# Hybrid encoder block: from GLU to the end, the low parts of weights and of the second norm's tiles are subtracted on VectorE instead of GpSimd

## The chip, the cores and the metric

The kernel runs on one core of one Trainium2 chip. The metric is the device time of one execution in microseconds, taken as the median of several runs. Everything is float32.

## The reference

One layer of an encoder block on 272 positions (16 meta tokens and 256 inputs) with 2048 features. All the heavy work is matrix products:

```python
hn = rms_norm(h, norm1_g)
q, k, v, u, g_na, g_ssm = split(hn @ w_in)
y_na = neighbourhood_attention(q, k, v, rpb) @ w_proj_na
y = gelu(s5(u)); y_ssm = (y * sigmoid(y @ w_glu)) @ w_proj_ssm
mixed = sigmoid(g_na) * y_na + sigmoid(g_ssm) * y_ssm
h = h + mixed @ w_out
a, g = split(rms_norm(h, norm2_g) @ w_up)
a = a[-1] * conv_w[0] + a[0] * conv_w[1] + a[+1] * conv_w[2] + conv_b   # along positions
h = h + (gelu(a) * g) @ w_down
return rms_norm(h, final_g)[:, 16:]
```

## The kernel before

Activations are kept with features on the partitions. To keep float32 precision every product is made of three: each operand is split into a high part (rounded to `fp32r`) and a low part (the difference), and TensorE adds high x high, low x high and high x low into PSUM.

**Units of weights.** Weights stream through three rings of four slots: `w_raw` (filled by SyncE's DMA queue), `w_hi` (ACT copies, `hi_unit`) and `w_lo` (a subtraction `w_raw - w_hi`, `lo_unit`, line 407). A unit is 128 x 1024 numbers, 512 KB, and takes TensorE 24 matmuls. The rings work like this: the load of a unit waits until the low part of the unit four before it is made (`s_lo`), its high part waits for the load and until TensorE has used the unit four before it (`s_used`), its low part waits for the high part (`s_hi`), and TensorE waits for the low part (`s_lo`). Until the end of attention the subtractions are shared between GpSimd and VectorE; from unit GLU 4 on all are GpSimd's, in the order of the units.

**Stages from GLU to the end**, in units: GLU 8, projections 32 (per half: two units of attention, two of `z`), `w_out` 32, up 176, down 88. `U_GLU`, `U_PROJ`, `U_OUT`, `U_UP`, `U_DOWN` are the numbers of the first units. The products of a stage are drained like this:

- GLU: ACT makes the sigmoid into `glu_ring` (line 879), VectorE multiplies (`mix_ring`, 1242), ACT makes `z_hi` (882), VectorE `z_lo` (1246). In the same stage ACT makes the sigmoids of the gates (872). The second product of the projections waits for all of `z_lo`.
- Projections: per block of four units VectorE makes four products with the gates (1256, 1258), two additions (1262) and, after ACT's high part (891), two subtractions (1266).
- After the last mix ACT starts the reload of the residual `xT` from DRAM (895), and VectorE waits for it (`s_xre`) ahead of its loop over `w_out`.
- `w_out`: per block of four units VectorE adds two tiles onto `xT` (1277), ACT squares them (579), TensorE sums the squares one block later (1371).
- Second norm: VectorE makes 1/rms in `rstd` (956, 961), then the 16 normed tiles in a ring of four (968), ACT the high parts (590), GpSimd the low parts (`norm_lo`, 421). VectorE starts on four tiles when GpSimd is done with the four before.
- Up: per block of eight units (four for the conv branch, four for the gate) ACT starts the conv (918), VectorE adds its two outer taps (1288, 1291), ACT makes gelu (926), VectorE multiplies by the gate (1297), ACT makes the high part (929), VectorE the low part (1302). PSUM holds two blocks, so TensorE waits for the products of line 1297 two blocks back. The down product begins when the last of them is done.

Of the kernel before, what the change touches and what calls it, by code (L numbers as in the profile page):

```python
# [22 lines left out]
SEED = 4  # L23
# [5 lines left out]
LIVE = N_META - 2  # L29
NL = L - LIVE  # L30
KT = D_MODEL // P
KH = HALF // P
FT = D_FF // P
DEPTH = 4
# [29 lines left out]
def encoder_block(nc, x, meta, norm1_g, w_in, rpb, lam_re, lam_im, log_step, b_re, b_im, c_re, c_im,  # L64
# [7 lines left out]
    ds = bass.ds  # L72
# [10 lines left out]
    with ctx:  # L83
# [380 lines left out]
        def _(pool):  # L464
# [85 lines left out]
            with pool.Fori(0, HEADS // 4) as i:  # L550
                for k in range(4):
# [5 lines left out]
                                .then_inc(s_bm, 1)  # L557
                    lo_unit(pool, (U_G + DEPTH + 4 * (G_SCAN + G_SSM)) + 8 * i, 2 * k)
                    lo_unit(pool, (U_G + DEPTH + 4 * (G_SCAN + G_SSM)) + 8 * i, 2 * k + 1)
            for k in range(8):  # L560
                lo_unit(pool, U_GLU + DEPTH, k)
            split_loop(pool, lo_unit, U_PROJ, 4, 8)
            split_loop(pool, lo_unit, U_OUT, 4, 8)
            norm_lo(pool, 1, NL)
            split_loop(pool, lo_unit, U_UP, FT // 4, 16)
            split_loop(pool, lo_unit, U_DOWN, FT // 2 - 1, 4)


        @block.scalar
# [377 lines left out]
        def _(dve):  # L947
# [5 lines left out]
            def norm(which, lo, n):  # L953

                dve.wait_ge(s_ss, which + 1)
                dve.tensor_scalar(rstd[:, 0:n], ps[:, 6, 0:n], 1.0 / D_MODEL, EPS, ALU.mult, ALU.add).then_inc(s_var, 1)
                if which == 0:
                    dve.wait_ge(s_gtp, 1)
                    dve.tensor_copy(gains[:, :], ps[:, 7, 0:2 * KT]).then_inc(s_gcp, 1)
                dve.wait_ge(s_sd, which + 1)  # L960
                dve.reciprocal(rstd[:, 0:n], rstd[:, 0:n])
                dve.drain()
                src = xT if which else x0T
                if which < 2:
                    with dve.Fori(0, KT // DEPTH) as i:
                        for k in range(DEPTH):
                            dve.wait_ge(s_nl, DEPTH * i + (KT * which + SEED))
                            dve.scalar_tensor_tensor(
                                out=tr[:, k, 0:n], in0=src[:, ds(DEPTH * i + k, 1), lo:lo + n].rearrange("p k n -> p (k n)"),
                                scalar=gains[:, ds(DEPTH * i + (KT * which + k), 1)], in1=rstd[:, 0:n],  # L970
                                op0=ALU.mult, op1=ALU.mult).then_inc(s_nt, 1)

            norm(0, 0, L)


# [259 lines left out]
                              anh[:, :, 0:2].bitcast(F), ALU.subtract).then_inc(s_mal, 1)  # L1235


            for n in range(KH):
                dve.wait_ge(s_sg, n + 1)
                if n >= 4:  # L1240
                    dve.wait_ge(s_zl, n - 3)
                dve.tensor_tensor(mt[:, n % 4, :], yT[:, n, LIVE:L], gt[:, n % 4, :], ALU.mult).then_inc(s_z, 1)
                if n % 4 == 3:
                    for m in range(n - 3, n + 1):
                        dve.wait_ge(s_zh, m + 1)
                        dve.tensor_tensor(zl[:, m, :], mt[:, m % 4, :], zh[:, m, :].bitcast(F), ALU.subtract).then_inc(s_zl, 1)
# [3 lines left out]
            dve.wait_ge(s_zl, KH)  # L1250
            with dve.Fori(0, 4) as i:
                for k in range(2):
                    dve.wait_ge(s_used, 8 * i + (U_PROJ + 4 * (k + 1)))
                    for m in range(2):
                        f = 4 * i + (2 * k + m)
# [15 lines left out]
            dve.wait_ge(s_xre, 16)  # L1271
            with dve.Fori(0, 4) as i:
                for k in range(2):
                    dve.wait_ge(s_used, 8 * i + (U_OUT + 4 * (k + 1)))
                    for m in range(2):
                        h = xT[:, ds(4 * i + (2 * k + m), 1), LIVE:L].rearrange("p k n -> p (k n)")
                        last = dve.tensor_tensor(h, h, ps[:, 2 * k + m, 0:NL], ALU.add)
                    last.then_inc(s_h1, 1)
            norm(1, LIVE, NL)


            with dve.Fori(0, FT // 4) as i:
                for k in range(2):
                    for m in range(2):
                        f = 4 * i + (2 * k + m)
                        dve.wait_ge(s_c, f + 1)
                        c = cv[:, k, m, :]
                        dve.scalar_tensor_tensor(out=c, in0=ps[:, 4 * k + m, 1:NL - 1], scalar=cvw[:, ds(f, 1)], in1=c,  # L1288
                                                 op0=ALU.mult, op1=ALU.add)
                        dve.drain()  # L1290
                        dve.scalar_tensor_tensor(out=cv[:, k, m, 0:SEQ - 1], in0=ps[:, 4 * k + m, 3:NL],
                                                 scalar=cvw[:, ds(f + 2 * FT, 1)], in1=cv[:, k, m, 0:SEQ - 1],
                                                 op0=ALU.mult, op1=ALU.add).then_inc(s_cd, 1)
                    dve.wait_ge(s_used, 16 * i + (U_UP + 8 * (k + 1)))
                    for m in range(2):
                        dve.wait_ge(s_ge, 4 * i + (2 * k + m + 1) + SEED)
# [7 lines left out]
                                          ALU.subtract).then_inc(s_fl, 1)  # L1304


            for m in range(0, KT, 2):
                dve.wait_ge(s_used, U_END - 1 if m < KH else U_END)
                h = xT[:, m:m + 2, N_META:L]
                dve.tensor_tensor(h, h, ps[:, m // 2, :].rearrange("p (a b) -> p a b", a=2), ALU.add).then_inc(s_h2, 1)  # L1310
# [388 lines left out]
```

## Time and profile before

| | |
|---|---|
| timed runs | 1756.8 us median of 3 (1756.56 to 1758.4) |
| profiled execution | span 1754.1 us from the first to the last instruction |
| around the span | 2.7 us between the span and the median |
| granted TensorE clock, mean | 0.952 of full speed |
| TensorE matmul busy | 1588.3 us (91%) |
| GpSimd busy | 1228.6 us (70%) |
| ACT busy | 808.9 us (46%) |
| VectorE busy | 595.1 us (34%) |

PE is TensorE, PEld its weight loads, DVE is VectorE, POOL is GpSimd, SP is SyncE. Busy shares are means over stages with different limits. An idle time in brackets is that of the engine ahead of the instruction, with what ended it. The stretch that the change touches runs from about 745 us to the end.

### The profile page before, as it was taken

To read this page: it belongs to the slowest core of one execution; us is meant where nothing else is said; L and a number is where in the kernel's file an instruction comes from. 1 tells how busy PE (TensorE), PEld (TensorE's weight loads), DVE (VectorE), ACT (ScalarE), POOL (GpSimd) and SP (SyncE) were. 2 spreads that over 40 slices of the span, in tenths; PEclk is the share of its full clock that TensorE was granted. 3 is DMA by queue.
4 is the path that set the end of the run, shared out by engine and by line. 5 is a ranking of instruction groups with operands and counts; after the bars stand their busy time and mean duration, and the time that the engine had idled before them with its cause. 6 is when DMAs were issued, how large, how long until landed. Compare 5 with 4: busy or idle time off the path is not lost.

```text
span 1754.1 us, 36211 instructions
## 1 busy us (share of the span) xinstructions
PE 1588.3 (91%) x12943; PEld 1539.5 (88%) x12943; DVE 595.1 (34%) x1171; ACT 808.9 (46%) x1351; POOL 1228.6 (70%) x698
## 2 busy tenths in 40 slices
PE   5589899992199899999999799999999999999997
PEld 3589899992199788799999799999999999999996
DVE  3019487897788333324400211111111111000002
ACT  3485333341077544464444555555555554333333
POOL 2567775783065366568887788888888888888883
PEclk9799899996599899999999899999999999999999
DMA  5544534652011354445665365555565555555552
GB/s 186 114 144 128 161 112 147 185 162 88 0 38 36 117 155 146 138 133 179 211 200 168 114 186 181 184 185 179 180 184 181 181 182 189 193 182 189 182 190 96
DMA packets 252903, 267.78 MB, mean 153 GB/s; under 512 B 38109, under 2 KB 240381, under 8 KB 252205
## 3 DMA queue, kind: packets, MB, share of 16 engines
q1 hardware_dynamic: 220496, 251.69, 45.9%
q10 hardware_dynamic: 32284, 15.27, 3.4%
q8 instruction: 33, 0.54, 0.1%
q14 instruction: 26, 0.21, 0.0%
q0 software_dynamic: 64, 0.07, 0.0%
HBM read 259.33 MB, written 9.52 MB: 153 GB/s over the span
## 4 chain that ended last, share of the span: by engine, by line
PE 76%; DVE 9%; issue 4%; POOL 3%; ACT 3%; DVEq 3%; DMA 1%; SPq 1%; ACTq 0%; POOLq 0%
PE ps L1343 17%; PE ps L1345 17%; PE ps L1344 17%; PE ps L1654 5%; PE ps L1656 5%; PE ps L1655 5%; DVE scan_states L1130 3%; DVE scan_t L993 3%; DVE scan_states L1132 2%; POOL w_lo L407 2%; PE ps L1509 2%; DVEq L1129 2%; PE ps L1451 2%; PE ps L1545 1%; PE ps L1443 1%
## 5 line engine op out<-in xcount | busy, mean ns | idle before, releaser
L407 POOL TENSOR_TENSOR w_lo<-w_raw,w_hi 128x1024 fp32r<-128x1024 f32 x440 | 1055.7, 2410 | 334.6 <-ACT w_hi L403 333.6
L1343 PE MATMUL ps<-act_hi,w_hi 128*128 128x258 f32 (+2 forms) x2688 | 780.9, 291 | 53.5 <-POOL w_lo L407 22.8
L403 ACT ACTIVATE w_hi<-w_raw 128x1024 fp32r<-128x1024 f32 x464 | 488.9, 1059 | 659.3 <-PE ps L1345 447.7
L1345 PE MATMUL ps<-act_hi,w_lo 128*128 128x258 f32 (+2 forms) x2688 | 770.4, 287 | 0.0
L1344 PE MATMUL ps<-act_lo,w_hi 128*128 128x258 f32 (+2 forms) x2688 | 769.2, 286 | 0.0
L1343 PEld LDWEIGHTS ps<-act_hi,w_hi 128*128 128x128 f32 x2688 | 517.9, 193 | 71.5 <-issue 37.5
L1344 PEld LDWEIGHTS ps<-act_lo,w_hi 128*128 128x128 f32 x2688 | 518.9, 193 | 0.2
L1345 PEld LDWEIGHTS ps<-act_hi,w_lo 128*128 128x128 f32 x2688 | 516.8, 192 | 0.0
L1654 PE MATMUL ps<-hidden_hi,w_hi 128*128 (+1 forms) x704 | 198.0, 281 | 2.2 <-DVE gelu_ring L1297 2.2
L1655 PE MATMUL ps<-hidden_lo,w_hi 128*128 (+1 forms) x704 | 197.1, 280 | 0.0
L1656 PE MATMUL ps<-hidden_hi,w_lo 128*128 (+1 forms) x704 | 197.0, 280 | 0.0
L1654 PEld LDWEIGHTS ps<-hidden_hi,w_hi 128*128 128x128 f32 x704 | 132.8, 189 | 2.5 <-DVE gelu_ring L1297 2.5
L1656 PEld LDWEIGHTS ps<-hidden_hi,w_lo 128*128 128x128 f32 x704 | 133.0, 189 | 0.0
L1655 PEld LDWEIGHTS ps<-hidden_lo,w_hi 128*128 128x128 f32 x704 | 132.4, 188 | 0.0
L435 POOL TENSOR_TENSOR t_p<-pow_out,c_slots 128x160 f32<-128x160 f32 x64 | 29.7, 494 | 101.2 <-PE ps L1509 101.0
L1297 DVE TENSOR_TENSOR gelu_ring<-gelu_ring,ps 128x256 f32<-128x256 f32 x44 | 16.6, 418 | 214.4 <-ACT gelu_ring L926 214.4
L1310 DVE TENSOR_TENSOR xT<-xT,ps 128x512 f32<-128x512 f32 x8 | 5.0, 683 | 246.0 <-PE ps L1656 246.0
L1288 DVE SCALAR_TENSOR_TENSOR conv_ring<-ps,conv_params,conv_ring 128x256 f32<-128x256 f32 x44 | 21.1, 480 | 190.6 <-ACT conv_ring L918 190.6
L1488 PE MATMUL ps<-g_nat,b_masked 128*32 128x96 f32 x128 | 17.5, 264 | 71.5 <-DVE g_nat L441 68.8
L1488 PEld LDWEIGHTS ps<-g_nat,b_masked 128*32 128x32 f32 x128 | 11.6, 117 | 73.6 <-issue 71.8
L435 POOL TENSOR_TENSOR t_p<-pow_in,b_bar 128x128 f32<-128x128 f32 x64 | 39.9, 651 | 22.5 <-PE ps L1443 22.5
L1130 DVE TENSOR_TENSOR scan_states<-scan_states,scan_t 128x128 f32 (+1 forms) x67 | 44.9, 671 | 13.2 <-issue 13.1
(230 smaller groups left out, 1873.3 us busy)
## 6 DMA issues: line engine op xcount, KB each, us to landing
w_raw<-in_w_up SPq DMA_DIRECT2D x176, 512.0 KB, 3.5
w_raw<-in_w_in SPq DMA_DIRECT2D x128, 512.0 KB, 3.8
w_raw<-in_w_down SPq DMA_DIRECT2D x88, 512.0 KB, 3.5
w_raw<-in_w_out SPq DMA_DIRECT2D x32, 512.0 KB, 3.4
w_raw<-in_w_proj_na SPq DMA_DIRECT2D x16, 512.0 KB, 3.4
w_raw<-in_w_proj_ssm SPq DMA_DIRECT2D x16, 512.0 KB, 3.4
w_raw<-in_w_glu SPq DMA_DIRECT2D x8, 512.0 KB, 3.5
bias_ring<-skew_scratch ACTq DMA_DIRECT2D x32, 96.0 KB, 2.6
```

The costliest lines, as they stand in the source:

```text
L403: act.activation(slot(whi, k), slot(raw, k), ACT.Copy).then_inc(s_hi, 1)
L407: pool.tensor_tensor(slot(wlo, k), slot(raw, k), slot(whi, k).bitcast(F), ALU.subtract).then_inc(s_lo, 1)
L435: eng.tensor_tensor(o[:, :, r, :, :], powers[:, dq, part, :].unsqueeze(3).to_broadcast(full), tab[:, dq, at_slot + r, :].unsqueeze(2).to_b ...
L993: dve.tensor_tensor(o, a, b, ALU.mult)
L1129: dve.drain()
L1130: dve.tensor_tensor(after, after, sc1[:, :], ALU.add)
L1343: mm(o, slot(whi, k)[:, cols], xh[:, kt, lo:lo + n], start=kt == 0, stop=False)
L1344: mm(o, slot(whi, k)[:, cols], xl[:, kt, lo:lo + n], start=False, stop=False)
L1345: ins = mm(o, slot(wlo, k)[:, cols], xh[:, kt, lo:lo + n], start=False, stop=kt == units * UKT - 1)
L1654: mm(o, slot(whi, k)[:, cols], xh, start=first and g % 2 == 0, stop=False, skip_group_check=True)
L1655: mm(o, slot(whi, k)[:, cols], xl, start=False, stop=False, skip_group_check=True)
L1656: ins = mm(o, slot(wlo, k)[:, cols], xh, start=False, stop=final, skip_group_check=True)
```

## The change

GpSimd's subtractions from unit GLU 4 on, and its 16 of the second norm, are taken out; VectorE makes them at places of its own program that are written out by hand: in GLU four ahead of each half, in the projections and in `w_out` four at the start of each block, in the up stage four at the start of each block and four between the conv and the gate, in the down stage in a loop of their own. The second norm's tiles are no longer a loop of four: product `k` and the low part of tile `k - 1` alternate.

```diff
-            for k in range(8):
-                lo_unit(pool, U_GLU + DEPTH, k)
-            split_loop(pool, lo_unit, U_PROJ, 4, 8)
-            split_loop(pool, lo_unit, U_OUT, 4, 8)
-            norm_lo(pool, 1, NL)
-            split_loop(pool, lo_unit, U_UP, FT // 4, 16)
-            split_loop(pool, lo_unit, U_DOWN, FT // 2 - 1, 4)
...
+            def norm_lo_tile(k, n):
+                dve.wait_ge(s_nh, KT + k + 1)
+                dve.tensor_tensor(hnl[:, k, 0:n], tr[:, k % DEPTH, 0:n], hnh[:, k, 0:n].bitcast(F), ALU.subtract)\
+                   .then_inc(s_nl, 1)
+            def norm_tiles(lo, n):
+                for k in range(KT):
+                    if k >= DEPTH:
+                        dve.wait_ge(s_nl, KT + k - DEPTH + 1 + SEED)
+                    dve.scalar_tensor_tensor(out=tr[:, k % DEPTH, 0:n], in0=xT[:, k, lo:lo + n],
+                                             scalar=gains[:, KT + k:KT + k + 1], in1=rstd[:, 0:n],
+                                             op0=ALU.mult, op1=ALU.mult).then_inc(s_nt, 1)
+                    if k:
+                        norm_lo_tile(k - 1, n)
+                norm_lo_tile(KT - 1, n)
...
+            dve.wait_ge(s_lo, U_GLU + DEPTH)
             for n in range(KH):
+                if n % 4 == 0:
+                    for k in range(n, n + 4):
+                        lo_unit(dve, U_GLU + DEPTH, k)
                 dve.wait_ge(s_sg, n + 1)
...
             with dve.Fori(0, 4) as i:
                 for k in range(2):
+                    for n in range(4):
+                        lo_unit(dve, (U_PROJ + DEPTH) + 8 * i, 4 * k + n)
                     dve.wait_ge(s_used, 8 * i + (U_PROJ + 4 * (k + 1)))
...
             dve.wait_ge(s_xre, 16)
             with dve.Fori(0, 4) as i:
                 for k in range(2):
+                    for n in range(4):
+                        lo_unit(dve, (U_OUT + DEPTH) + 8 * i, 4 * k + n)
                     dve.wait_ge(s_used, 8 * i + (U_OUT + 4 * (k + 1)))
...
             norm(1, LIVE, NL)
+            norm_tiles(LIVE, NL)
...
             with dve.Fori(0, FT // 4) as i:
                 for k in range(2):
+                    for n in range(4):
+                        lo_unit(dve, (U_UP + DEPTH) + 16 * i, 8 * k + n)
                     for m in range(2):
...
+                    for n in range(4, 8):
+                        lo_unit(dve, (U_UP + DEPTH) + 16 * i, 8 * k + n)
                     dve.wait_ge(s_used, 16 * i + (U_UP + 8 * (k + 1)))
...
+            split_loop(dve, lo_unit, U_DOWN, FT // 2 - 1, 4)
```

VectorE's program at the start of the loop over `w_out`, before the change (`L1272` is the loop's head, which waits for the reload of `xT`; `xT<-xT,ps` are the additions to the residual):

```order
L1272 UNCONDITIONAL_BRANCH
L1272 ISA
L1277 ISA
L1277 TENSOR_TENSOR xT<-xT,ps 128x258
L1277 ISA
L1277 TENSOR_TENSOR xT<-xT,ps 128x258
```

The same place of the changed kernel, where the loop's head is `L1288` and the additions are `L1295`:

```order
L1288 UNCONDITIONAL_BRANCH
L1288 ISA
L407 TENSOR_TENSOR w_lo<-w_raw,w_hi 128x1024
L406 REGISTER_ALU
L407 TENSOR_TENSOR w_lo<-w_raw,w_hi 128x1024
L406 REGISTER_ALU
L407 TENSOR_TENSOR w_lo<-w_raw,w_hi 128x1024
L406 REGISTER_ALU
L407 TENSOR_TENSOR w_lo<-w_raw,w_hi 128x1024
L1292 REGISTER_ALU
L1295 ISA
L1295 TENSOR_TENSOR xT<-xT,ps 128x258
```

Four weight subtractions, which stood on GpSimd, now stand between the wait for the reload and the first addition.

VectorE's program in the second half of a block of the up stage, before the change (the gate products and the low parts of the hidden tiles; just ahead of it are the conv's operations):

```order
L1294 REGISTER_ALU
L1296 REGISTER_ALU
L1297 TENSOR_TENSOR gelu_ring<-gelu_ring,ps 128x256
L1296 REGISTER_ALU
L1297 TENSOR_TENSOR gelu_ring<-gelu_ring,ps 128x256
L1302 ISA
L1302 TENSOR_TENSOR hidden_lo<-gelu_ring,hidden_hi 128x256
```

The same place of the changed kernel (`L1320` are the gate products, `L1325` the low parts):

```order
L406 REGISTER_ALU
L407 TENSOR_TENSOR w_lo<-w_raw,w_hi 128x1024
L406 REGISTER_ALU
L407 TENSOR_TENSOR w_lo<-w_raw,w_hi 128x1024
L406 REGISTER_ALU
L407 TENSOR_TENSOR w_lo<-w_raw,w_hi 128x1024
L1319 REGISTER_ALU
L1320 TENSOR_TENSOR gelu_ring<-gelu_ring,ps 128x256
L1319 REGISTER_ALU
L1320 TENSOR_TENSOR gelu_ring<-gelu_ring,ps 128x256
L1325 ISA
L1325 TENSOR_TENSOR hidden_lo<-gelu_ring,hidden_hi 128x256
```

The last weight subtraction of a block, whose high part waits until the block's last unit is used, now stands ahead of the gate products.

## Rows read from the trace of the kernel before

**Rows 1.** The page, part 1: busy us, share of the span, instructions.

```profile
PE 1588.3 (91%) x12943; PEld 1539.5 (88%) x12943; DVE 595.1 (34%) x1171; ACT 808.9 (46%) x1351; POOL 1228.6 (70%) x698
```

**Rows 2.** Waits of TensorE, 745 us to the end: total us, times, longest.

```profile
PE ps L1343 <- POOL act_lo L421: 10.3, 3, 7.8
PE ps L1343 <- DVE z_lo L1246: 2.5, 1, 2.5
PE ps L1654 <- DVE gelu_ring L1297: 2.2, 1, 2.2
```

**Rows 3.** Groups by line and form, 745 us to the end.

```profile
L407 POOL TENSOR_TENSOR w_lo<-w_raw,w_hi 128x1024 fp32r<-128x1024 f32 x332 | 794.3, 2403 | 173.5 <-ACT w_hi L403 173.5
L1302 DVE TENSOR_TENSOR hidden_lo<-gelu_ring,hidden_hi 128x256 f32 x44 | 26.7, 646 | 8.3 <-ACT hidden_hi L929 8.3
L1262 DVE TENSOR_TENSOR mix_ring<-mix_ring,glu_ring 128x258 f32<-128x258 f32 x16 | 23.6, 1513 | 0.6
```

**Rows 4.** Line 407 on VectorE, before 600 us: ns min/median/max.

```profile
L407 DVE TENSOR_TENSOR w_lo<-w_raw,w_hi x24: 1214/1225/1254, 201.8 to 579.4; 128x1024 fp32r<-128x1024 f32 x24
```

**Rows 5.** Timeline of GLU and the projections' start: start us, duration us.

```profile
760.25 2.03 DVE L1242 TENSOR_TENSOR mix_ring<-y_ssm,glu_ring 128x258 f32<-128x258 f32 x4 [8.98 <-ACT glu_ring L879]
...
774.15 1.66 DVE L1242 TENSOR_TENSOR mix_ring<-y_ssm,glu_ring 128x258 f32<-128x258 f32 x4 [10.51 <-ACT glu_ring L879]
775.73 1.43 DVE L1246 TENSOR_TENSOR z_lo<-mix_ring,z_hi 128x258 fp32r<-128x258 f32 x4
...
777.29 0.58 PE L1343 MATMUL ps<-z_hi,w_hi 128*128 128x258 f32 x1 [2.55 <-DVE z_lo L1246]
```

**Rows 6.** Reload of `xT`: timeline, a 2 us window, a transfer to landing.

```profile
870.63 0.34 ACTq L895 DMA_DIRECT2D xT<-xT_scratch  x1
877.19 1.06 ACT L403 ACTIVATE w_hi<-w_raw 128x1024 fp32r<-128x1024 f32 x1 [1.87 <-PE ps L1345]
...
879.39 0.76 DVE L1277 TENSOR_TENSOR xT<-xT,ps 128x258 f32 x2 [7.91 <-DMA xT<-xT_scratch]
...
872.40 9.47 POOL L407 TENSOR_TENSOR w_lo<-w_raw,w_hi 128x1024 fp32r<-128x1024 f32 x4 [2.35 <-ACT w_hi L403]
...
874.00:876.00 2.00, 2.00 (x19) 2.00 (x18) 0.00 (x0) 1.06 (x1) 2.00 (x2) 1.00 0.99 418
...
xT_scratch<-x_feature_major SPq DMA_DIRECT2D x1, 2176.0 KB, 6.6
```

**Rows 7.** Timeline around the second norm.

```profile
962.86 1.06 ACT L403 ACTIVATE w_hi<-w_raw 128x1024 fp32r<-128x1024 f32 x1 [1.81 <-PE ps L1345]
963.96 0.73 ACT L579 ACTIVATE square_ring<-xT 128x258 f32 x2
...
968.85 1.68 DVE L968 SCALAR_TENSOR_TENSOR norm_ring<-xT,gains,rstd 128x258 f32<-128x258 f32 x4 [0.47 <-issue]
...
983.90 3.13 POOL L421 TENSOR_TENSOR act_lo<-norm_ring,act_hi 128x258 f32 x4 [1.48 <-ACT act_hi L590]
...
973.42 0.58 PE L1343 MATMUL ps<-act_hi,w_hi 128*128 128x258 f32 x1 [7.84 <-POOL act_lo L421]
...
982.55 0.38 PE L1343 MATMUL ps<-act_hi,w_hi 128*128 128x258 f32 x1 [0.94 <-POOL act_lo L421]
...
987.16 0.38 PE L1343 MATMUL ps<-act_hi,w_hi 128*128 128x258 f32 x1 [1.48 <-POOL act_lo L421]
```

**Rows 8.** Windows: TensorE, its loads, VectorE, ACT, GpSimd busy; clock; DMA share; GB/s.

```profile
777.00:777.50 0.50, 0.21 (x1) 0.22 (x2) 0.16 (x1) 0.50 (x2) 0.22 (x1) 0.50 0.67 232
...
780.50:781.00 0.50, 0.50 (x6) 0.50 (x5) 0.00 (x0) 0.00 (x0) 0.50 (x1) 1.00 0.19 37
```

**Rows 9.** Timeline at the end of the up stage.

```profile
1482.12 1.06 ACT L403 ACTIVATE w_hi<-w_raw 128x1024 fp32r<-128x1024 f32 x1 [1.82 <-PE ps L1345]
1485.00 1.06 ACT L403 ACTIVATE w_hi<-w_raw 128x1024 fp32r<-128x1024 f32 x1 [1.81 <-PE ps L1345]
...
1486.39 0.75 DVE L1297 TENSOR_TENSOR gelu_ring<-gelu_ring,ps 128x256 f32<-128x256 f32 x2 [9.06 <-ACT gelu_ring L926]
```

More of the change, by code:

```diff
@@ L962, in norm @@
                 dve.drain()
-                src = xT if which else x0T
-                if which < 2:
+                if which == 0:
                     with dve.Fori(0, KT // DEPTH) as i:
                         for k in range(DEPTH):
-                            dve.wait_ge(s_nl, DEPTH * i + (KT * which + SEED))
+                            dve.wait_ge(s_nl, DEPTH * i + SEED)
                             dve.scalar_tensor_tensor(
-                                out=tr[:, k, 0:n], in0=src[:, ds(DEPTH * i + k, 1), lo:lo + n].rearrange("p k n -> p (k n)"),
-                                scalar=gains[:, ds(DEPTH * i + (KT * which + k), 1)], in1=rstd[:, 0:n],
+                                out=tr[:, k, 0:n], in0=x0T[:, ds(DEPTH * i + k, 1), lo:lo + n].rearrange("p k n -> p (k n)"),
+                                scalar=gains[:, ds(DEPTH * i + k, 1)], in1=rstd[:, 0:n],
                                 op0=ALU.mult, op1=ALU.mult).then_inc(s_nt, 1)
+            def norm_lo_tile(k, n):
[12 more added lines that the diff above has]
+                norm_lo_tile(KT - 1, n)
             norm(0, 0, L)
```

## The prediction, made before the changed kernel was run

> **What bounds the kernel now.** I read the page first. In its busy times [rows 1] TensorE is at 91% of the span, GpSimd at 70%, VectorE at 34%. That GpSimd is busy says nothing yet; the question is who waits for it. So the second view is the list of waits from 745 us to the end, the stretch that the change touches [rows 2]. TensorE has only three waits there that are worth anything: 10.3 us in three pieces for `act_lo` of GpSimd (all at the second norm), 2.5 us for `z_lo` of VectorE (between GLU and the projections), 2.2 us for `gelu_ring` of VectorE (between the up and the down product). There is no wait of TensorE for `w_lo` in it. The 332 weight subtractions of GpSimd, 2.40 us each and 794 us together [rows 3], are all hidden: one unit of weights takes TensorE 2.88 us (the starts 1482.12 and 1485.00 of two `w_hi` that each waited for it [rows 9]), and the low part of a unit is needed four units after its slot comes free. So only edges of stages can change, where TensorE waits or can be made to.
>
> **What the change costs and saves as such.** It takes 332 + 16 subtractions off GpSimd and puts them into VectorE's queue. The price on VectorE is in this trace: 24 weight subtractions already run there, 1.214 to 1.254 us each [rows 4]. I take 1.23. That is 332 x 1.23 = 408 us more on an engine busy 595 us of 1754: it does not become a bound on average. In the up stage a block of four units lasts 4 x 2.88 = 11.5 us and gets 4 x 1.23 = 4.9 us of new work. What matters is order: VectorE works in order, so a subtraction can now stand behind a wait of VectorE, and a VectorE operation can stand behind a subtraction. I go through the four edges.
>
> **GLU: about -0.8 us.** VectorE's four products of the first half take 2.03 us, those of the second 1.66 us, while four subtractions of the same size with GpSimd idle take 1.43 us [rows 5]. The `mix_ring` addition shows the same: 1513 ns mean [rows 3], where the first of a pair ends only after the GpSimd operation that was running. With GpSimd silent both fours should take 1.43 us: 0.60 + 0.23 = 0.8 us. The first gain is passed on because ACT goes from `z_hi` through four `w_hi` and four gates to the next `glu_ring` with hardly a gap, and `z_lo`, which ends at 775.73 + 1.43 = 777.16, is what TensorE waits for (777.29, idle 2.55 us [rows 5]). The new subtractions ahead of these products do not delay them: the fourth needs a `w_hi` that ACT makes before `glu_ring` in its own queue. The bounds are 0 (ACT sets the pace) and -0.85.
>
> The Trainium skill (SBUF — State Buffer, Terms) calls the port pair of VectorE and GpSimd an exclusive lock held for a full instruction. These rows agree with a block, not with shared speed.
>
> **Reload of xT: about +2.0 us.** This is the new wait. VectorE waits for `s_xre` ahead of the loop over `w_out`, and the subtractions for its units 4 to 7 now stand behind that wait. Today the reload is issued at 870.63 and VectorE starts at 879.39, while GpSimd had begun with unit 4 at 872.40 [rows 6]. Unit 3 was used up at 877.19 (the `w_hi` that waited for it), less the 0.1 us of the hand-over and the tail: TensorE wants the low part of unit 4 at 877.0. If the reload lands as today, it is there at 879.39 + 1.23 = 880.6: a stall of 3.6 us. But today the reload shares the DMA engines with weight loads, at 418 GB/s in all [rows 6]; these loads wait for slots that the late subtraction no longer frees. 2.23 MB at 418 GB/s are 5.3 us, and the transfer of the same size to `xT_scratch` took 6.6 us in all [rows 6], which gives 877.2, VectorE 0.3 us later, low part at 878.8: a stall of 1.8 us. The issue itself stays where it is: the last mix of the projections waits 2.3 us more (w_hi 1.06, subtraction 1.23), and its pair of additions gets back about the same 2.2 us (2 x 1.5 against 2 x 0.42). I take 2.0, nearer the fast end, because nothing else is left to load; the ends are 1.0 and 3.6. Units 5 to 7 then follow at 1.23 us against TensorE's 2.88, so nothing later waits.
>
> **Second norm: about -1.2 us.** Two things oppose. First, VectorE's last pair of h additions stands behind the fourth subtraction: `w_hi` starts at 962.86 and takes 1.06, the subtraction 1.23, the additions 0.76 (as at 879.39 [rows 6]), so the squares start at 966.05 instead of 963.96 [rows 7]: +2.1, and all that follows moves by it; the first norm tile goes from 968.85 to 970.95. Second, the tiles get faster. Today the four groups of four last from 968.85 to 983.90 + 3.13 = 987.03, 4.5 us each, since VectorE waits for all four of GpSimd's. Afterwards each tile costs one product (1.68/4 = 0.42 us) and one subtraction (1.43/4 = 0.36 us), interleaved: 0.78 us a tile. The last low part is there at 970.95 + 15 x 0.78 + 1.5 (product, ACT's high part, subtraction, two hand-overs) = 984.2, against 987.03. TensorE can't take all of these 2.8 us. It starts on the first four tiles at 973.42 today and about 975.1 afterwards (970.95 + 3 x 0.78 + 1.6, and 0.2), and its first unit after the idle time of 7.84 us is slow: 973.42 to 982.55 less 0.94 idle, less a tail of 0.28 and a full-speed unit of 2.88, leaves 5.0 us, as after the GLU stall, where the granted clock is 0.50, 1.2 of 2.4 GHz [rows 8]. So its fourth unit starts at 975.1 + 5.0 + 2 x 2.88 = 985.9, with its tiles ready, instead of 987.16 [rows 7]: -1.2. If product and subtraction don't overlap (0.48 + 0.42 = 0.90 a tile) it is -1.0; at 1.1 us a tile nothing is gained and 0.4 lost. If the clock recovers a little earlier it is -1.9.
>
> **Up to down: +0.9 us.** The last high part starts at 1485.00, so the subtraction runs from 1486.15 to 1487.35, and the last gelu products of VectorE start behind it instead of at 1486.39 [rows 9]. TensorE, idle 2.24 us for them today [rows 2], waits 0.9 us more. Inside the up stage the same delay is hidden: TensorE needs those products one whole block (11.5 us) later. The down stage has only subtractions on VectorE. The tail is as before.
>
> **Clock.** In the 2.55 us of idle time ahead of 777.29 the granted clock fell to 0.50, and it was back at 1.00 by 780.50 [rows 8]. Half speed over 3.3 us costs 1.6 us. With the GLU stall down to 1.7 us that fall may go (-1.6); with a new stall of 2.0 us at 877 a new one may come (+1.6). About even for the first, two in three for the second. I take one fall of the two: net zero.
>
> **Sum.** -0.8 + 2.0 - 1.2 + 0.9 = +0.9 us on a profiled span of 1754.1 us. The timed runs have a median of 1756.8 us, 2.7 above the span, which I carry over: 1757.7, say 1757.8. About 0.2% (3.5 us, 1753.3 to 1760.3) is what a measurement of this kernel can tell from no change.
>
> **Rivals.**
> 1. The reload decides, slower. It takes its 8.8 us in spite of the quieter DMA engines: stall 3.6, and the clock falls, 1.6 more. With -0.8 - 1.2 + 0.9 that is +4.1: 1760.9. It decides once stall and clock together cost over 4.6 us. For it: the row 879.39. Against it: 418 GB/s moved, of which the reload alone is only 2.23 MB. Chance 0.17.
> 2. Faster: the GLU stall no longer drops the clock (-1.6), the reload is hidden (it would have to land by 875.5), and the norm gives its full 2.8 because the clock is back sooner: -0.8 - 1.6 - 2.8 + 0.9 = -4.3, 1752.5. With the reload at its lower end of 1.0 it is -3.3, just inside the 0.2%. For it: each step is within the bounds above. Against it: all must hold together. Chance 0.10.
> 3. The lock on every pair is worth its sum: `mix_ring` 16 x (1.51 - 0.42) = 17 us and `hidden_lo` 44 x (0.65 - 0.42) = 10 us [rows 3], 27 us off: 1730. Against it: TensorE never waits for either. Chance 0.03. The Trainium skill (SBUF — State Buffer, Terms) lets the loser of the lock block fully; by that rule alone one would expect these 27 us.
> 4. The order on VectorE makes TensorE wait in every block of the up stage, say 0.5 us in each of 22: +11, 1769. A subtraction can be held by conv (2 us) or the gelu chain (1.35 us from high part to product [rows 9], then 1.1 us) and still has over 5 of its 8.6 us (three units) left. Chance 0.05.
>
> **How the numbers follow.** Forecast (within 0.2%) 0.65; the others as given. Faster 0.12, same 0.66, slower 0.22. The ends: all terms at their good ends without rival 3 give about 1753.5; rival 1 with no gain at the norm 1762.1. So 1753.7 to 1762.0; the forecast's own range is 1754.5 to 1760.
>
> **What would show it.** `w_lo` on VectorE at 1.23 us, 356 of them. `mix_ring` additions near 0.42 us. TensorE idle for a `w_lo` once, near 877 us, 1 to 3.6 us. TensorE's idle time ahead of `z_hi` 1.7 us. Norm tiles on VectorE every 0.78 us, and one wait of TensorE for `act_lo` at most after the first. An idle time near 3.1 us before the down product. Wrong would be: waits of TensorE for `w_lo` that repeat each block, `w_lo` well above 1.25 us, or no gap at all at the reload.

## The result, and the profile after

The changed kernel takes 1761.62 us in the median of 20 runs, against 1755.43 us for 20 runs of the kernel before: a ratio of 1.003, 95% interval 1.0023 to 1.0037. It is slower by 5.3 us (4.0 to 6.5 us by the ends of the interval); the two medians lie 6.2 us apart. The time lies inside the predicted range, at its slow end, and not in the case that was forecast as likeliest (no change that can be measured): it came out as the first rival had it. Three runs far above the rest of their kernel are left out of the comparisons: 6366 us here, and among the experiments 2442 us (e1) and 1840.8 us (the kernel before).

The page of the profiled execution, its span and part 1, against [rows 1]:

```profile
span 1759.5 us, 36055 instructions
PE 1588.4 (90%) x12943; PEld 1540.1 (88%) x12943; DVE 970.9 (55%) x1519; ACT 806.4 (46%) x1351; POOL 420.4 (24%) x350
```

TensorE does the same work (1588.4 us against 1588.3) in a span that is 5.4 us longer. All of the difference is idle time or slow clock. The groups from 745 us to the end (by line and form: busy us, mean ns of one, idle before them) answer to [rows 3]:

```profile
L407 DVE TENSOR_TENSOR w_lo<-w_raw,w_hi 128x1024 fp32r<-128x1024 f32 x332 | 404.6, 1225 | 431.4 <-ACT w_hi L403 422.0 <-DMA xT<-xT_scratch 9.4
L1325 DVE TENSOR_TENSOR hidden_lo<-gelu_ring,hidden_hi 128x256 f32 x44 | 16.8, 422 | 8.3 <-ACT hidden_hi L922 8.3
L1278 DVE TENSOR_TENSOR mix_ring<-mix_ring,glu_ring 128x258 f32<-128x258 f32 x16 | 6.1, 424 | 0.6
```

The price of the subtraction is as predicted, 1225 ns. The two other lines have lost their blocking: 1513 to 424 ns and 646 to 422 ns. And the first row names the new wait: 9.4 us of VectorE's idle time ahead of `w_lo` end with the reload of `xT`. TensorE's own waits in the same stretch, against [rows 2] (total us, times, longest):

```profile
PE ps L1367 <- DVE act_lo L968: 6.8, 1, 6.8
PE ps L1367 <- DVE w_lo L407: 4.9, 1, 4.9
PE ps L1678 <- DVE gelu_ring L1320: 3.1, 1, 3.1
PE ps L1395 <- ACT square_ring L572: 2.8, 1, 2.8
PE ps L1367 <- DVE z_lo L1260: 1.9, 1, 1.9
```

Three of them changed as foretold: `act_lo` from three waits to one, `gelu_ring` from 2.2 to 3.1 us, `z_lo` from 2.5 to 1.9 us. `w_lo` is the new one. The wait for `square_ring` was 0.7 us in the kernel before:

```profile
PE ps L1371 <- ACT square_ring L579: 0.7, 1, 0.7
```

Its 2.1 us more are the foretold delay of the last additions to `xT`, which stand behind a subtraction. The timeline around the reload, against [rows 6]:

```profile
870.03 0.34 ACTq L888 DMA_DIRECT2D xT<-xT_scratch  x1
876.82 1.06 ACT L403 ACTIVATE w_hi<-w_raw 128x1024 fp32r<-128x1024 f32 x1 [1.87 <-PE ps L1369]
...
880.29 4.63 DVE L407 TENSOR_TENSOR w_lo<-w_raw,w_hi 128x1024 fp32r<-128x1024 f32 x4 [9.41 <-DMA xT<-xT_scratch]
...
881.66 0.55 PE L1367 MATMUL ps<-act_hi,w_hi 128*128 128x258 f32 x1 [4.94 <-DVE w_lo L407]
```

The windows of the same time (TensorE, its loads, VectorE, ACT, GpSimd busy, then granted clock, DMA share, GB/s):

```profile
877.00:878.00 1.00, 0.00 (x0) 0.00 (x0) 0.00 (x0) 0.87 (x1) 0.00 (x0) 1.00 0.26 104
878.00:879.00 1.00, 0.00 (x0) 0.00 (x0) 0.00 (x0) 0.00 (x0) 0.00 (x0) 1.00 0.08 35
879.00:880.00 1.00, 0.00 (x0) 0.00 (x0) 0.00 (x0) 0.00 (x0) 0.00 (x0) 0.71 0.08 35
...
885.00:886.00 1.00, 1.00 (x7) 1.00 (x6) 0.59 (x2) 0.19 (x1) 0.00 (x0) 0.50 0.90 290
886.00:887.00 1.00, 1.00 (x9) 1.00 (x9) 0.00 (x0) 0.69 (x3) 0.00 (x0) 0.88 0.90 181
```

TensorE had used up unit 3 at 876.7 and waited until 881.66, because the low part of unit 4 stood behind the wait for the reload. From 877 on nothing but the last of the reload was moving, at 104 and then 35 GB/s; it landed at 880.1. During the stall the granted clock fell to 0.50, and TensorE worked at half speed until 886.

**Where the 5.4 us went.** I take four points on TensorE in each trace: the first matmul with `z_hi`, the first of `w_out`, the last group of four that sums the second norm's squares, the first of the down product. The stretches between them, in us, and the reload's time from issue to landing:

| | first `z_hi` at | to `w_out` | to last square sum | to down | to the end | reload |
|---|---|---|---|---|---|---|
| before | 777.29 | 88.13 | 99.01 | 522.77 | 266.9 | 8.4 |
| changed | 776.76 | 88.29 | 108.33 | 519.18 | 267.0 | 10.1 |
| e1 | 775.31 | 88.29 | 101.10 | 519.28 | 267.0 | 8.2 |
| e2 | 777.08 | 86.80 | 105.98 | 522.76 | 267.0 | 8.2 |
| e3 | 775.09 | 88.31 | 99.01 | 518.41 | 265.5 | 8.4 |
| e4 | 775.41 | 88.31 | 99.01 | 518.80 | 267.3 | 10.2 |
| e5 | 779.03 | 88.29 | 108.45 | 519.16 | 267.0 | 4 parts, last 8.9 |
| e6 | 775.70 | 88.25 | 99.09 | 520.15 | 268.1 | 10.9 |
| e7 | 775.53 | 86.81 | 99.08 | 519.30 | 266.9 | 10.8 |
| e8 | 774.71 | 86.79 | 99.02 | 522.75 | 267.0 | 8.4 |
| e9 | 775.06 | 86.80 | 107.88 | 519.33 | 257.7 | 9.4 |
| e10 | 775.95 | 86.79 | 101.11 | 519.28 | 267.0 | 8.9 |
| e11 | 778.02 | 88.28 | 108.50 | 519.55 | 265.5 | 8.0 |

The first column holds mostly what the change doesn't touch; it scatters by 4 us between executions. For the changed kernel the differences to before are -0.53, +0.16, +9.32, -3.59 and +0.1: together +5.5, the whole of it (5.4 between the spans as the pages round them). The rows e1 to e11 are the experiments.

Two columns also hold a clock effect that differs between executions and must not be read as an effect of a kernel: the second column (88.1 to 88.3, or 86.8, taken up below) and the last. Ahead of the down product TensorE waits 2.2 or 3.1 us; in most executions the granted clock then falls to 0.50 for three microseconds or so, but in e3 (2.24 us) and e11 (3.07 us) it stayed at 1.00, which gives the 265.5 of these two rows, and in e6 it stayed low longer, which gives 268.1. e11 just after its wait:

```profile
1495.00:1496.00 1.00, 1.00 (x11) 1.00 (x10) 0.42 (x2) 0.00 (x0) 0.00 (x0) 1.00 0.94 365
1496.00:1497.00 1.00, 1.00 (x11) 1.00 (x10) 0.00 (x0) 0.00 (x0) 0.00 (x0) 1.00 0.79 193
```

### The profile page after: what moved, and what is told of

It reads as the page before. It is cut to its first block, busy times and chain, and to the rows that moved or that the text cites. A ratio compares the mean times of both kernels' runs of the same rounds, so it can differ in the third digit from the quotient of the medians.

```text
span 1759.5 us, 36055 instructions
## 1 busy us (share of the span) xinstructions
PE 1588.4 (90%) x12943; PEld 1540.1 (88%) x12943; DVE 970.9 (55%) x1519; ACT 806.4 (46%) x1351; POOL 420.4 (24%) x350
## 4 chain that ended last, share of the span: by engine, by line
PE 77%; DVE 9%; issue 4%; ACT 3%; POOL 2%; DVEq 2%; DMA 1%; SPq 1%; ACTq 0%; POOLq 0%
PE ps L1367 18%; PE ps L1369 17%; PE ps L1368 17%; PE ps L1678 5%; PE ps L1680 5%; PE ps L1679 5%; DVE scan_states L1140 3%; DVE scan_t L1003 3%; POOL w_lo L407 2%; PE ps L1533 2%; DVE scan_states L1142 2%; PE ps L1475 2%; DVEq L1139 1%; PE ps L1569 1%; PE ps L1467 1%
## 5 line engine op out<-in xcount | busy, mean ns | idle before, releaser
L407 DVE TENSOR_TENSOR w_lo<-w_raw,w_hi 128x1024 fp32r<-128x1024 f32 x356 | 434.0, 1225 | 435.4 <-ACT w_hi L403 423.1
L407 POOL TENSOR_TENSOR w_lo<-w_raw,w_hi 128x1024 fp32r<-128x1024 f32 x108 | 260.2, 2422 | 162.8 <-ACT w_hi L403 162.0
L1140 DVE TENSOR_TENSOR scan_states<-scan_states,scan_t 128x128 f32 (+1 forms) x67 | 53.4, 796 | 13.2 <-issue 13.1
L1003 DVE TENSOR_TENSOR scan_t<-scan_states,chunk_re 128x128 f32<-128x128 f32 x67 | 50.8, 759 | 10.4 <-issue 6.2
L1202 DVE SCALAR_TENSOR_TENSOR scores<-ps,bias_ring 128x256 f32<-128x256 f32 x32 | 12.1, 420 | 72.2 <-POOL bias_ring L555 40.9
```

Of the source, the lines that this page charges most:

```text
L407: pool.tensor_tensor(slot(wlo, k), slot(raw, k), slot(whi, k).bitcast(F), ALU.subtract).then_inc(s_lo, 1)
L1003: dve.tensor_tensor(o, a, b, ALU.mult)
L1140: dve.tensor_tensor(after, after, sc1[:, :], ALU.add)
```

## The experiments

The theory: the loss is the wait of VectorE for the reload with four weight subtractions behind it, worth its stall of 4.9 us and a fall of the clock. The rival: VectorE's additional work as such, or its order elsewhere, is what costs. Ratios are to the kernel before on the same chip.

**e1: the wait behind the subtractions.**

```diff
-            dve.wait_ge(s_xre, 16)
             with dve.Fori(0, 4) as i:
                 for k in range(2):
                     for n in range(4):
                         lo_unit(dve, (U_OUT + DEPTH) + 8 * i, 4 * k + n)
+                    dve.wait_ge(s_xre, 16)
```

> The changed kernel, with VectorE's wait for the reload of xT behind the four weight subtractions of each w_out block instead of ahead of the loop. Theory (the reload wait, with the clock fall behind it, is the loss: 7.2 us between the kernels' traces): no idle time of TensorE near 877 us, no half clock there, span near 1752 to 1753, ratio to before 0.998 to 0.999. Rival (VectorE's extra work or its order costs it elsewhere and the stall only moved the loss): ratio stays at 1.002 to 1.003.

Measured: 1753.41 us, ratio 0.9981 (0.9967 to 0.9995). TensorE has no wait for `w_lo` any more, and the stretch from `w_out` to the last square sum is 101.10 us instead of 108.33. One wait moved by four instructions is worth 7.2 us in the trace and turns the change from a loss into a small gain. The rival falls as the cause of these 7.2 us: all 332 subtractions are still on VectorE.

**e2: the same wait in the kernel before, on GpSimd.**

```diff
+            pool.wait_ge(s_xre, 16)
             split_loop(pool, lo_unit, U_OUT, 4, 8)
```

> The kernel before, with one wait added: GpSimd waits for the reload of xT ahead of its w_out subtractions. Nothing is moved to VectorE. Theory (the loss is the wait as such): TensorE idles for w_lo once near 877 us, until the reload's landing plus 2.4 us of subtraction; 5 to 7 us of idle time and about 2 us for the clock, ratio 1.003 to 1.005. Rival (the loss belongs to VectorE's queue): ratio 1.000.

Measured: 1762.51 us, ratio 1.0039 (1.0025 to 1.0054). TensorE's waits from 745 us in this kernel:

```profile
PE ps L1344 <- POOL act_lo L421: 10.1, 3, 7.8
PE ps L1344 <- POOL w_lo L407: 4.4, 1, 4.4
PE ps L1344 <- DVE z_lo L1247: 2.5, 1, 2.5
PE ps L1655 <- DVE gelu_ring L1298: 2.2, 1, 2.2
```

All is as in the kernel before [rows 2] but for one wait of 4.4 us, and the third stretch grew by 6.97 us (105.98 against 99.01). So the loss is made without VectorE. The expected 5 to 7 us of idle time were a little too many, since the reload landed 8.2 us after its issue here, and the 2.6 us beyond the wait (6.97 less 4.4) are a little more than the 2 us allowed for the clock.

**e3: the norm's tiles alone on VectorE.** The kernel before with `norm_tiles` in place of the loop of four and of GpSimd's `norm_lo`; all weight subtractions stay on GpSimd.

```diff
             split_loop(pool, lo_unit, U_OUT, 4, 8)
-            norm_lo(pool, 1, NL)
             split_loop(pool, lo_unit, U_UP, FT // 4, 16)
...
             norm(1, LIVE, NL)
+            norm_tiles(LIVE, NL)
```

> The kernel before, with only the second norm's low parts on VectorE, tile by tile; all weight subtractions stay on GpSimd. In the changed kernel the norm stage gave 2.3 us net of a delay of about 2.1 us ahead of it, which is not there here. Theory: the tile chain gives 4 us or a little more, TensorE waits once for act_lo, about 4 us less than now in all; ratio 0.9975 to 0.998. Rival (TensorE's cold first unit eats what the tiles give): 2 us, ratio 0.999.

Measured: 1749.81 us, ratio 0.997 (0.9959 to 0.9981). In the trace the stretch from the last square sum to the down product shrinks by 4.36 us, as the theory had it, and not by the rival's 2 us. This part of the change alone is a clear gain.

**e4: the subtractions of the w_out stage back on GpSimd.**

```diff
+            pool.wait_ge(s_lo, U_OUT + DEPTH)
+            split_loop(pool, lo_unit, U_OUT, 4, 8)
...
             with dve.Fori(0, 4) as i:
                 for k in range(2):
-                    for n in range(4):
-                        lo_unit(dve, (U_OUT + DEPTH) + 8 * i, 4 * k + n)
                     dve.wait_ge(s_used, 8 * i + (U_OUT + 4 * (k + 1)))
...
             norm_tiles(LIVE, NL)
+            dve.wait_ge(s_lo, U_UP + DEPTH)
```

> The changed kernel with the 32 subtractions of the w_out stage back on GpSimd, everything else as changed. This takes away both the reload wait (7.2 us) and the subtraction ahead of the last h additions (about 2.1 us). Theory: ratio 0.9965 to 0.998, no idle time for w_lo. Rival (the up and down stages on VectorE cost something): ratio at or above 1.000.

Measured: 1751.55 us, ratio 0.9981 (0.9968 to 0.9994). The third stretch is back at 99.01 us to the hundredth, though 300 of the 332 subtractions are still on VectorE: the two losses of this stretch (7.2 and 2.1 us) both come from the 32 of `w_out`. The reload took 10.2 us in this execution and cost nothing.

**e5: the reload in four transfers of four tiles.**

```diff
-            act.dma_start(xT[:, :, :].rearrange("p k t -> p (k t)"), xT_d).then_inc(s_xre, 16)
+            for n in range(4):
+                act.dma_start(xT[:, 4 * n:4 * n + 4, :].rearrange("p k t -> p (k t)"),
+                              xT_d[:, 4 * n * L:4 * (n + 1) * L]).then_inc(s_xre, 16)
...
-            dve.wait_ge(s_xre, 16)
+            dve.wait_ge(s_xre, 64)
```

> The changed kernel with the reload of xT issued as four transfers of four tiles each instead of one. In the changed kernel the reload landed 10.1 us after its issue, though the DMA engines were nearly silent (35 GB/s) for its last 3 us. Theory (one of the 16 DMA engines is late with its part of the one large transfer): smaller transfers spread anew, landing 1 to 2 us earlier, stall below 4 us, ratio 1.001 to 1.003. Rival (the reload's time is set by something else, such as reading DRAM that was just written): landing at 10 us as before, ratio 1.003.

Measured: 1759.27 us, ratio 1.0023 (1.0013 to 1.0033). The four parts were issued from 872.30 to 873.66 and landed 4.7 to 8.9 us after their own issue, the last of them 10.2 us after the first issue; TensorE waited 5.1 us. So nothing landed earlier, as the rival had it, and the stall is not below the 4 us of the theory. The windows of the last microseconds:

```profile
880.00:881.00 1.00, 0.00 (x0) 0.00 (x0) 0.00 (x0) 0.15 (x1) 0.00 (x0) 1.00 0.18 70
881.00:882.00 1.00, 0.00 (x0) 0.00 (x0) 0.00 (x0) 0.00 (x0) 0.00 (x0) 0.88 0.13 52
```

The slow end is there again, at 70 and 52 GB/s. In this one execution splitting the transfer didn't spread its end anew, so that explanation of it finds no support.

**e6: the additions ahead of the block's last subtraction** (e1 with this edit).

```diff
-                    for n in range(4):
+                    for n in range(3):
                         lo_unit(dve, (U_OUT + DEPTH) + 8 * i, 4 * k + n)
                     dve.wait_ge(s_xre, 16)
...
                     last.then_inc(s_h1, 1)
+                    lo_unit(dve, (U_OUT + DEPTH) + 8 * i, 4 * k + 3)
```

> As e1, and in each w_out block the two additions to xT stand ahead of the block's fourth subtraction. Theory: the squares of the last pair start about 2.1 us earlier, and 2 us more than in e1 are saved; ratio about 0.997. Rival (the norm chain is bounded by the table load of ACT or by TensorE's restart): below 1 us more than e1.

Measured: 1751.41 us, ratio 0.9979 (0.997 to 0.9987). The wait for `square_ring` is 0.8 us instead of e1's 2.8, and the third stretch 99.09 instead of 101.10: the delay of 2.0 us is the one subtraction and the high part that it waits for. Of these 2.0 us the trace of e6 loses 0.9 again in the fourth stretch (520.15 against 519.28). In the execution of e6 the clock stays low for longer after the wait of 6.8 us; TensorE restarts at 971.01 in e6 and at 970.39 in e3. First e6, then e3:

```profile
976.00:977.00 1.00, 1.00 (x7) 1.00 (x7) 1.00 (x4) 0.56 (x2) 0.00 (x0) 0.50 0.00 0
977.00:978.00 1.00, 1.00 (x9) 1.00 (x9) 1.00 (x4) 0.49 (x2) 0.00 (x0) 0.95 0.00 0
```

```profile
974.00:975.00 1.00, 1.00 (x8) 1.00 (x8) 1.00 (x4) 0.46 (x2) 0.00 (x0) 0.80 0.00 0
975.00:976.00 1.00, 1.00 (x11) 1.00 (x10) 1.00 (x4) 0.59 (x2) 0.00 (x0) 1.00 0.00 0
```

The ratio alone can't be told from that of e1. The order is shown by the stretch, not by the timed runs.

**e7: the gate products ahead of the block's last subtraction** (e6 with this edit).

```diff
-                    for n in range(4, 8):
+                    for n in range(4, 7):
                         lo_unit(dve, (U_UP + DEPTH) + 16 * i, 8 * k + n)
...
                            .then_inc(s_fm, 1)
+                    lo_unit(dve, (U_UP + DEPTH) + 16 * i, 8 * k + 7)
```

> As e6, and in each up block the gate products stand ahead of the block's last weight subtraction. Theory: the idle time of TensorE ahead of the down product falls from 3.07 to about 2.2 us, 0.8 us less than e6 in all; ratio 0.9965. Rival: the subtraction, now later, holds the first down unit and nothing is gained.

Measured: 1749.22 us, ratio 0.9957 (0.9943 to 0.9971), the lowest median of all. There are only six runs, one of them at 1741.98 us, and that one pulls the ratio down: the medians (1749.22 against 1755.21) are in a ratio of 0.9966. TensorE's waits from 745 us on, against those of the changed kernel:

```profile
PE ps L1369 <- DVE act_lo L968: 6.8, 1, 6.8
PE ps L1680 <- DVE gelu_ring L1321: 2.2, 1, 2.2
PE ps L1369 <- DVE z_lo L1260: 1.9, 1, 1.9
PE ps L1397 <- ACT square_ring L572: 0.8, 1, 0.8
```

The `gelu_ring` wait is back to 2.2 us, as it was before the change. The whole change is in this kernel; only the wait for the reload, and in each block one pair of additions or one pair of products, stand elsewhere in VectorE's queue.

Set beside e3, it also shows where the gain comes from. e3, which moves nothing but the 16 tiles of the norm, has a ratio of 0.997 (0.9959 to 0.9981), and the two intervals overlap. In the table its third and fourth stretches together are 4.36 us shorter than before, those of e7 3.40 us; e7's clock stayed low for over six microseconds after the restart at the norm (969.40 to past 975), as e6's did. So apart from the 0.7 us ahead of `z_hi` (e8), no trace here shows a gain from moving the 332 weight subtractions: placed well, they are free, and the norm's tiles are what pays.

**e8: the eight subtractions of GLU alone on VectorE** (the kernel before with this edit).

```diff
-            for k in range(8):
-                lo_unit(pool, U_GLU + DEPTH, k)
+            pool.wait_ge(s_lo, U_PROJ + DEPTH)
...
+            dve.wait_ge(s_lo, U_GLU + DEPTH)
...
+                if n % 4 == 0:
+                    for k in range(n, n + 4):
+                        lo_unit(dve, U_GLU + DEPTH, k)
```

> The kernel before with only the eight subtractions GLU 4 to projections 3 on VectorE; GpSimd does all the others. Theory (VectorE's products of the GLU stage are no longer blocked by GpSimd's subtractions): idle time of TensorE ahead of z_hi falls from 2.55 to about 1.9 us, 0.5 us in all, within noise; ratio 0.9995. Rival: nothing, as ACT's chain sets the pace, idle time 2.5 us.

Measured: 1754.56 us, ratio 0.9994 (0.9985 to 1.0002). The interval holds 1, so the timed runs don't tell it from no change. In the timeline the wait has shrunk from 2.55 us [rows 5]:

```profile
774.71 0.38 PE L1346 MATMUL ps<-z_hi,w_hi 128*128 128x258 f32 x1 [1.86 <-DVE z_lo L1249]
```

That is 0.69 us less, and the changed kernel has the same (1.85 us). By the theory it comes from VectorE's products no longer being blocked: the four of each half take 1.44 and 1.49 us here instead of 2.03 and 1.66.

**e9: the changed kernel once more**, nothing edited.

> The changed kernel once more, unchanged, for a second look at the reload. It landed in 8.2 to 8.4 us in five profiles (the kernel before and e1, e2, e3, e8) and in 10.1 to 10.9 us in four (the changed kernel, e4, e6, e7). If the landing is fixed by the kernel: 10.1 us and a stall of 4.9 us again. If it varies from run to run: as likely 8.3 us and a stall near 3.2 us.

Measured: 1759.47 us, ratio 1.002 (1.0011 to 1.003). Here the reload landed 9.4 us after its issue, not 10.1, and TensorE waited 4.25 us:

```profile
877.78 0.55 PE L1367 MATMUL ps<-act_hi,w_hi 128*128 128x258 f32 x1 [4.25 <-DVE w_lo L407]
```

So the landing varies between executions of one kernel. So does the clock after the GLU wait. In this execution it stayed at 1.00, and the second stretch lasted 86.80 us instead of 88.29, after the same wait of 1.9 us. The changed kernel's profile first, then e9's, at the first matmuls after the wait:

```profile
777.00:778.00 1.00, 1.00 (x6) 1.00 (x6) 1.00 (x1) 0.70 (x1) 0.00 (x0) 0.51 0.07 16
```

```profile
776.00:777.00 1.00, 1.00 (x11) 1.00 (x10) 1.00 (x2) 0.00 (x0) 0.00 (x0) 1.00 0.00 0
```

**e10: e1 once more**, nothing edited.

> The kernel of e1 once more, for its reload: it was the only one with the projections' subtractions on VectorE that landed in 8.2 us. If the landing is fixed by the kernel: 8.2 us again. If it varies: 10 to 11 us may come. No idle time near 877 us either way.

Measured: one run, 1752.85 us. The reload took 8.9 us (8.2 in e1) and TensorE had no idle time near 877 in either. The third stretch agrees with e1 to 0.01 us; the second differs by the same 1.5 us as between the changed kernel and e9.

**e11: the reload issued once no weight load is under way** (the changed kernel with this edit).

```diff
+            act.wait_ge(s_raw[(U_OUT + 7) % DEPTH], 16 * ((U_OUT + 7) // DEPTH + 1))
             act.dma_start(xT[:, :, :].rearrange("p k t -> p (k t)"), xT_d).then_inc(s_xre, 16)
```

> The changed kernel, with ACT waiting for the landing of the weights of w_out unit 7 (the last load under way) before it issues the reload, so that the reload has the DMA engines to itself. Theory (weights still under way on some engines make one of them late with its part): the reload is issued about 1 to 1.5 us later but lands in 6.5 to 7.5 us with no silent end, stall 3 to 4.5 us. Rival (the transfer is that uneven by itself): 10 us from issue to landing, a stall of 6 us or more.

Measured: 1759.62 us, ratio 1.0009 (0.998 to 1.0039). Three of its ten runs are short ones, of 1747.6 to 1748.9 us (see the last section), the others lie from 1757.2 to 1761.9, so the ratio says nothing. The trace says more:

```profile
872.82 0.34 ACTq L889 DMA_DIRECT2D xT<-xT_scratch  x1
```

```profile
873.00:874.00 1.00, 1.00 (x11) 1.00 (x10) 0.00 (x0) 0.54 (x1) 0.00 (x0) 1.00 1.17 226
874.00:875.00 1.00, 1.00 (x11) 1.00 (x10) 0.00 (x0) 1.00 (x2) 0.00 (x0) 1.00 0.27 52
875.00:876.00 1.00, 1.00 (x10) 1.00 (x10) 0.00 (x0) 1.00 (x2) 0.00 (x0) 1.00 1.02 418
876.00:877.00 1.00, 1.00 (x11) 1.00 (x10) 0.00 (x0) 0.41 (x1) 0.00 (x0) 1.00 0.85 366
877.00:878.00 1.00, 0.97 (x8) 0.75 (x7) 0.00 (x0) 0.00 (x0) 0.00 (x0) 1.00 1.17 505
878.00:879.00 1.00, 0.00 (x0) 0.00 (x0) 0.00 (x0) 0.93 (x1) 0.00 (x0) 1.00 0.89 383
879.00:880.00 1.00, 0.00 (x0) 0.00 (x0) 0.00 (x0) 0.12 (x1) 0.00 (x0) 1.00 0.65 279
880.00:881.00 1.00, 0.00 (x0) 0.00 (x0) 0.00 (x0) 0.00 (x0) 0.00 (x0) 1.00 0.00 0
```

Alone on the DMA engines the reload still takes 8.0 us, more than the 6.5 to 7.5 expected. These windows hold all of its 2.23 MB: 0.28 MB in a first burst and a pause up to 875, then 1.95 MB in the five microseconds to 880, at 390 GB/s and with no slow end. It landed at 880.84, 0.8 us later. The flow itself is close to the 418 GB/s of the prediction; the first two microseconds and the last 0.8 were not in its sum. TensorE waited 4.45 us, since the issue came 1.5 us later after the first matmul of `w_out` than in the changed kernel (6.5 us against 5.0).

## Why the time fell inside the range, and not in the likeliest case

The time lies 3.8 us above the forecast of 1757.8 and inside the stated range. Part of that nearness is luck. The forecast started from 1756.8 us, the median of three runs, where 20 runs give 1755.43: the change itself was forecast at +1.0 us and measured at +5.3 us. And two errors partly cancel, 5.2 us too little at the reload and 1.1 us too little gain at the norm. Term by term, against a profiled execution that lost 5.5 us where the sum had +0.9:

| term | predicted | measured | by |
|---|---|---|---|
| GLU wait | -0.8 | -0.7 | 1.85 - 2.55, the wait ahead of `z_hi`; the same in e8 |
| reload, stall and clock | +2.0 and 0 | +7.2 | 108.33 - 101.10 (e1) |
| additions behind the subtraction | +2.1 | +2.1 | 101.10 - 99.01 |
| norm tiles, after that delay | -3.3 | -4.4 | 518.41 - 522.77 (e3) |
| up to down | +0.9 | +0.8 | 3.07 - 2.24 |
| up stage, down stage, tail | 0 | +0.1 | last column |
| sum | +0.9 | +5.2 | |

The measured terms add to 5.2 (unrounded), against 5.5 in the trace; the 0.3 left are mostly 0.16 in the second stretch and 0.16 in the first column, which holds work that the change doesn't touch.

**The step that failed is the reload's term.** The place and the mechanism were as written: one wait of TensorE for `w_lo` near 877, because the subtractions of units 4 to 7 stood behind `s_xre`. e1, e2 and e4 show it from three sides: take the wait away from the subtractions, or the subtractions away from the wait, and the stall is gone; put the same wait ahead of GpSimd's subtractions in the kernel before, and 7.0 us are lost there. The issue stayed where it was (870.03), and the weight loads did stop, both as written. Wrong was that the reload would land at 877.2. I had worked from bytes over bandwidth and from the 6.6 us of the write to `xT_scratch`. e11 shows that even undisturbed this read lands 8.0 us after its issue; 8.2 to 10.9 us were seen in the other executions that left it whole. The reason given for the shorter time fell too. The window of 418 GB/s [rows 6] was read as the reload sharing the engines with weight loads, but it lies in a gap between them: of the two loads around it, the one issued at 870.22 landed 3.4 us later and the next was issued only at 874.97:

```profile
870.22 0.37 SPq L348 DMA_DIRECT2D w_raw<-in_w_out  x1
...
874.97 0.37 SPq L348 DMA_DIRECT2D w_raw<-in_w_out  x1
```

With the loads gone, the reload took 10.1 and 9.4 us in the two executions of the changed kernel, against 8.4 in the kernel before. The row of the kernel before, 8.8 us from issue to VectorE's start [rows 6], was the better price, and even that was short: 870.03 + 8.8 would be 878.8, and VectorE started at 880.29.

**The clock step failed beside it.** "One fall of the two, net zero" traded two events that weren't alike. After the stall of 4.9 us the clock fell and stayed at 0.50 until 886; 7.2 less the stall of 4.9 leaves 2.3 us for it, more than the 1.6 allowed; it is what about 4.4 us at half speed cost (881.66 to past 886). The fall after the GLU wait, which was to go in exchange, comes in some executions and not in others, with a wait of 1.9 us (changed kernel and e9) and of 2.5 us alike: e2 waited those 2.5 us and lost no clock.

```profile
777.00:778.00 1.00, 0.93 (x7) 0.93 (x8) 0.00 (x0) 0.94 (x1) 0.93 (x1) 1.00 0.14 49
```

So that fall is worth 1.5 us in an execution (88.3 against 86.8) but it isn't a difference between these kernels that a single profile may be read for.

**The norm came out right, and larger.** The delay ahead of it was 2.1 us, as worked out. The tiles on VectorE came every 0.73 us and not 0.78:

```profile
978.48 0.43 DVE L968 TENSOR_TENSOR act_lo<-norm_ring,act_hi 128x258 fp32r<-128x258 f32 x1 [0.19 <-ACT act_hi L583]
...
989.47 0.43 DVE L968 TENSOR_TENSOR act_lo<-norm_ring,act_hi 128x258 fp32r<-128x258 f32 x1 [0.25 <-ACT act_hi L583]
```

(989.47 - 978.48 is 15 pitches.) TensorE waited once for `act_lo`, 6.84 us, and then never again, as foretold. e3 puts the gain at 4.4 us instead of 3.3. Of it 1.0 is the first wait (7.84 to 6.84), 2.4 are the two waits that are gone (0.94 and 1.48 [rows 7]), and some 0.5 is the clock, which was at half speed for 5 us after the restart before and for 4 in e3; the last 0.5 us I can't assign. The net of delay and gain is -2.3 us, beyond the best end that the prediction gave this term (-1.9).

**The rivals.** Rival 1, the reload decides, is what happened: it needed 4.6 us of stall and clock and got 7.2. Its own price, 5.2, was 2 us short for the reason above. Rival 2 falls: it needed the reload hidden. Its norm term was 2.8 net, 2.3 were measured. With the reload hidden, as e1 has it, the time was 1753.4 us, near its 1752.5. Rival 3, the sum of the blocking, falls. The blocking was real: `mix_ring` went from 1513 to 424 ns and `hidden_lo` from 646 to 422 ns. Yet in the changed kernel, where all of it is gone, the stretches that hold these rows got no shorter (88.29 us against 88.13 for the projections; none beyond the norm's terms in the up stage), because TensorE never waited for them. The only such gain is the 0.7 us ahead of `z_hi`, where it did wait. The Trainium skill (SBUF — State Buffer, Terms) says that the loser of the port lock fully blocks; these rows agree with it (one of each pair of `mix_ring` additions took 2.3 to 2.6 us beside GpSimd's subtractions of 2.40 us, where the other took 0.4 to 0.6; without them both took 0.42 us), and the kernel's time doesn't follow from it. Rival 4, a wait in every block of the up stage, falls: between 1000 and 1480 us TensorE has no wait at all in the changed kernel.

**Argued, not shown; and open.** That the rest of the sum closes to 0.3 us is read from single profiled executions, whose reload varies by 0.7 us between two of the same kernel. Why the last part of the reload crawls at 35 GB/s in the changed kernel, at 52 in e5, and not at all in e11, is open. In e11 no other load was beside it and in e5 cutting it up was no cure, each in one execution; but other loads alone don't bring it either, since e1 had them and landed in 8.2 us. The seven whole reloads of kernels with the projections' subtractions on VectorE took 8.2 to 10.9 us, six of them 8.9 or more; the four with those on GpSimd took 8.2 to 8.4. That points at what precedes the reload, but no run takes that apart.

## What to carry to other kernels

When work moves to an engine that has time, list the waits that it will stand behind, not the busy share. Here about 400 us of new work cost and gained next to nothing as such, and one wait with four subtractions behind it cost 7.2 us. Put a wait on a transfer right ahead of the first instruction that uses its data, and the instruction that another engine waits for ahead of work that nobody needs yet; with three such moves the same change goes from 1.003 to 0.9957 (0.9966 by medians). Try the parts of a change alone: the norm's tiles by themselves gave nearly all of that. And price a transfer by a row that runs from its issue to its first reader, since bytes over bandwidth left out the time ahead of the flow and behind it, and an uneven end.

## What was unexpected of the hardware

- After one and the same wait of 1.9 us the granted clock fell to 0.50 in one execution of the changed kernel and stayed at 1.00 in another, worth 1.5 us. A wait of 3.07 us (e11, before the down product) left it at 1.00 too. After the reload's stalls of 4.3 to 5.1 us it fell each time.
- The reload of 2.23 MB landed 8.0 to 10.9 us after its issue, 9.4 and 10.1 in two executions of one kernel.
- Some executions are 7 to 13 us shorter than the median of the rest of their kernel: three in the kernel before (1744.87 to 1746.6 us), one each in e1, e7 and e9, three in e11. e9's profile caught one: the down stage lasted 257.7 us instead of 266.9, at a granted clock of 1.00 in both. The same window in the changed kernel's profile and in e9's holds 427 and 444 matmuls, 117.1 and 112.6 ns each:

```profile
1500.00:1550.00 50.00, 50.00 (x427) 50.00 (x426) 21.66 (x18) 19.07 (x18) 0.00 (x0) 1.00 0.55 185
```

```profile
1500.00:1550.00 50.00, 50.00 (x444) 50.00 (x443) 22.81 (x19) 19.36 (x19) 0.00 (x0) 1.00 0.58 196
```

What makes TensorE 4% faster there at the same granted clock, no run here shows. It is as large as all that this study is about, and a reason to time a kernel more than once.
